# Attention loop of a hybrid diffusion step: row sums behind the first value visit, the inverse behind the fourth maximum, GpSimd's first addition behind two value products

## The chip, the cores and the metric

The kernel runs on one core of a Trainium2 chip. The metric is the device time of one execution, in microseconds (us). The median of three runs of the kernel before is 2347.97 us.

## The reference, cut to what matters

The reference is one layer of a hybrid backbone with three token mixers beside each other, followed by an output projection and a feed-forward part. The change touches only the attention mixer of the 1024 latent tokens. They are swept in 8 blocks of 128 queries; each block reads 1152 keys (1024 latent ones and 128 cached ones) with 8 query heads that share 2 key/value heads.

```python
def one(qblk):
    s = jnp.einsum('bqkgd,bskd->bkgqs', qblk, k).astype(jnp.float32) * scale
    p = jax.nn.softmax(s, axis=-1).astype(v.dtype)
    return jnp.einsum('bkgqs,bskd->bqkgd', p, v)
```

The softmax needs, for each query and head, a maximum over the keys, the exponentials, their sum (the row sum) and its inverse.

## The kernel before, in words

All work of the attention stage is in the function `attention` (L1876). Each engine has its own program, a list of instructions in a fixed order, and the engines meet only through semaphores. The order on each engine is written out by hand. The loop runs over tiles i = 0 to 7 (`LAST` is 7), one for each block of 128 queries. While tile i computes exponentials and products, TensorE already computes the scores that give the maxima of tile i + 1.

**TensorE** (`tile`, L2239). `head(h)` (`shift_scores`, three matmuls, L2165) fills PSUM banks 0 to 2 with the scores of head h of the next tile; it waits until the maximum of the head before has been taken. `steps` (`scores`, L2188 and L2189) makes the 18 transposed score blocks m = 0 to 17 of this tile, in three rotating banks, each freed by an exponential. `queries` and `shifts` (L2068 and L2073) turn the operands of a later tile through the one bank `PT`. `values(i, g)` (L2202) multiplies three blocks of exponentials with the values: this is one visit, there are three in a tile, and a visit has three products of two key/value heads each. `sums(i - 1)` (L2209) adds the exponentials of the previous tile over the keys, into the bank `PT`. `spread_sums(i - 1)` (L2235) spreads their inverse over the output rows. In the kernel before, `sums(i - 1)` stands between `head(2)` and `values(i, 0)`.

**VectorE** (`tile`, L2561). For each head it takes the maximum (L2531, reads PSUM). Between the maxima stand `next_split` (L2494 and L2495), which prepares the operands that `queries` turns; `norm_b` (L2489); `inverted` (L2537, the reciprocal of the row sums, reads the bank `PT`), in the kernel before after the third maximum (h = 2); `normed` (L2543) and `norm_a` (L2481, L2483, L2485) after the sixth; and in the last tile `ahead` (L2549, L2552), low parts of operands of the next stage.

**GpSimd** (`add_trio`, L2038). It adds the three blocks of exponentials a, b and c of a visit into c, so that TensorE has a third of the sums to make. The first addition (L2042) waits for the whole visit, the second (L2046) for the first, and in two visits of three also for a split of VectorE (`part`). Between the additions it runs `rope` (L2032 to L2035) and `inverse_norm` (L2023).

**ScalarE** (`tile`, L2388) takes the exponentials (L2379), copies turned operands out of `PT` (L2360, L2364), copies out the output (L2386), and in tiles 6 and 7 makes the high parts of operands of the next stage (`ahead`, L2409, L2412), after the exponentials 7, 13 and 17.

Who may write the bank `PT` is set by waits. The one that matters here is in `shifts`:

```python
if kv == 0 and i >= 2:
    pe.wait_ge(sem["rc"], i - 1)
```

Called as `shifts(i + 1, 0)` behind `head(4)`, it waits until `inverted(i - 1)` of this same tile has read the row sums.

Of the kernel before, what the change touches and what calls it, by code (L numbers as in the profile page):

```python
# [17 lines left out]
ALU = mybir.AluOpType  # L18
# [1857 lines left out]
def attention(nc, g):  # L1876
# [14 lines left out]
    TRIO, SLOTS = 3, 4  # L1891
    LASTG = (LAT // P) * NT // TRIO - 1
    LAST = LAT // P - 1
    fill = g.fill
    with Phase(nc, "att") as ph:
# [26 lines left out]
        ones, spread = ph.sb("ones", [P, 32]), ph.sb("spread", [P, G, HD])  # L1922
# [4 lines left out]
        with ExitStack() as later:  # L1927
            trio += [later.enter_context(nc.sbuf_tensor(f"att_trio{i}", [P, KV, G * P], F32)) for i in range(2, SLOTS)]
        b0st = [ph.sb(f"b0st{i}", [P, TH]) for i in range(STAGES)]
        names = ("load qload const knd kpow kout ktm kte qd qpow rope cpart qtm qte csmm cmx cex cptm cpte comm cdone "  # L1930
                 "part s1 mx ptm pte s2 ex pv paired sums rc spread norm evict yout0 yout1 kv dve mly mlw mlhi b0y1 b0y2 b0w b0yh b0wh b0yl b0wl b0mm b0ev b0out0 b0out1 b0out2 b0out3 b0out4 b0out5 b1lo")
        sem = {n: ph.sem(n) for n in names.split()}
        block = ph.block()
        PT, ST, OB = 3, 4, 7
# [1 line left out]
        def held(n):  # L1936

            b, r = divmod(n, TRIO)
            return trio[b % SLOTS] if r == TRIO - 1 else pt[b % 2 * 2 + r]
# [73 lines left out]
        @block.gpsimd  # L2013
        def _(gp):
            gp.memset(khalf[:], -0.5).then_inc(sem["const"], 1)
            gp.memset(va[:, :, :, HD:H1], 1.0).then_inc(sem["const"], 1)
            gp.memset(ones[:], 1.0).then_inc(sem["const"], 1)
            gp.wait_ge(sem["const"], 1)
            gp.wait_ge(sem["knd"], 3)
            gp.tensor_tensor(krs[:], kms[:], khalf[:], ALU.pow).then_inc(sem["kpow"], 1)  # L2020
            def inverse_norm(n):
                gp.wait_ge(sem["qd"], 4 * n + 3)
                gp.tensor_tensor(qrs[:], qms[:], khalf[:, 0:AH], ALU.pow).then_inc(sem["qpow"], 1)  # L2023

            def rope(n, e):

                gp.wait_ge(sem["qd"], 4 * n + 4 + 4)
                x = qn[:].rearrange("p h (d e) -> p h d e", e=2)
                o = qr[:].rearrange("p h (d e) -> p h d e", e=2)
                w = lambda c: qtab[:, n, c, :].unsqueeze(1).broadcast_to([P, AH, HD // 2])  # L2030
                a, b = (0, 1) if e == 0 else (2, 3)
                gp.tensor_tensor(u1[:], x[:, :, :, 0], w(a), ALU.mult).then_inc(sem["rope"], 1)  # L2032
                gp.tensor_tensor(u2[:], x[:, :, :, 1], w(b), ALU.mult).then_inc(sem["rope"], 1)
                gp.wait_ge(sem["rope"], 6 * n + 3 * e + 2)
                gp.tensor_tensor(o[:, :, :, e], u1[:], u2[:], ALU.subtract if e == 0 else ALU.add).then_inc(sem["rope"], 1)  # L2035
                gp.wait_ge(sem["rope"], 6 * n + 3 * e + 3)

            def add_trio(n, split=None):  # L2038

                a, b, c = (held(TRIO * n + x) for x in range(TRIO))  # L2040
                gp.wait_ge(sem["pv"], n + 1)
                gp.tensor_tensor(c[:], c[:], a[:], ALU.add).then_inc(sem["paired"], 1)  # L2042
                gp.wait_ge(sem["paired"], 2 * n + 1)
                if split is not None and split[0] <= LAST:
                    gp.wait_ge(sem["part"], 2 * split[0] + split[1] + 1)
                gp.tensor_tensor(c[:], c[:], b[:], ALU.add).then_inc(sem["paired"], 1)  # L2046

            inverse_norm(0)
            for n in range(2):
                inverse_norm(n + 1)  # L2050
                for e in range(2):
                    rope(n, e)
            inverse_norm(3)
            for i in range(LAST + 1):
                if i:
                    add_trio(3 * i - 1, (i + 1, 1))
                if i + 2 <= LAST:
                    rope(i + 2, 0)
                add_trio(3 * i)
                if i + 2 <= LAST:  # L2060
                    rope(i + 2, 1)
                add_trio(3 * i + 1, (i + 2, 0))
                if i + 3 <= LAST:
                    inverse_norm(i + 4)
# [12 lines left out]
        def _(pe):  # L2077
# [28 lines left out]
            n = 0  # L2106
            for part in range(2):
                rows = (P, H1)[part]
                for kv in range(KV):
                    for t0, nt in ((0, 4), (4, 4), (8, 2)):  # L2110
                        if n >= 6:
                            pe.wait_ge(sem["kte"], n - 5)
                        for t in range(nt):
                            mm = pe.transpose(ps[0:rows, n % 6, t * P:t * P + P],
                                              kpart[part][:, t0 + t, kv, :].bitcast(F32), g.ident[:])
# [75 lines left out]
            def values(i, g):  # L2191

                if g == 0:
                    if i:
                        pe.wait_ge(sem["evict"], i)
                    else:
                        pe.wait_ge(sem["b0ev"], 24)
                for j in range(TRIO * g, TRIO * g + TRIO):
                    n = NT * i + j
                    pe.wait_ge(sem["ex"], 2 * n + 2)  # L2200
                    for kv in range(KV):
                        mm = pe.matmul(ps[kv * HD:kv * HD + HD, OB, :], va[:, j, kv, 0:HD], held(n)[:, kv, :],  # L2202
                                       start=j == 0, stop=j == NT - 1)
                mm.then_inc(sem["pv"], 1)

            def add(x, first, last):
# [32 lines left out]
            def tile(i):  # L2239

                more = i < LAST

                def steps(first, last):
                    for m in range(first, last):
                        scores(i, m % KV, m // KV)

                def head(h):
                    if more:
                        shift_scores(i + 1, h)

                shifts(i, 1)
                head(0)
                steps(0, 4)
                head(1)
                if more:
                    queries(i + 1, 1)
                steps(4, 7)
                head(2)
                if i:
                    sums(i - 1)  # L2260
                values(i, 0)
                head(3)
                steps(7, 11)
                head(4)
                if more:
                    shifts(i + 1, 0)
                steps(11, 14)
                head(5)
                if i:
                    spread_sums(i - 1)  # L2270
                values(i, 1)
                head(6)
                steps(14, 18)
                head(7)
                if i + 2 <= LAST:
                    queries(i + 2, 0)
                values(i, 2)
# [29 lines left out]
        def _(act):  # L2307
# [80 lines left out]
            def tile(i):  # L2388
                more = i < LAST
                shifts(i, 1)  # L2390
                for m in range(2 * NT):
                    if more and m == 4:
                        queries(i + 1, 1)
                    if more and m == 11:
                        shifts(i + 1, 0)
                    exponentials(i, m // KV, m % KV)
                    if i >= LAST - 1 and m in (7, 13, 17):
                        ahead(3 * (i - LAST + 1) + (7, 13, 17).index(m))
                if i + 2 <= LAST:
                    queries(i + 2, 0)  # L2400
                output(i)

            def ahead(n):
                if n == 0:
                    act.wait_ge(sem["mly"], 64)
                if n == 4:
                    act.wait_ge(sem["mlw"], 32)
                if n < 4:
                    act.activation(g.ys0[:, n, :], g.ys0[:, 4 + n, :].bitcast(F32), ACT.Copy).then_inc(sem["mlhi"], 1)  # L2409
                else:  # L2410
                    b = n - 4
                    act.activation(g.wt[:, b, :], g.wraw[:, 2048 * b:2048 * b + 2048], ACT.Copy).then_inc(sem["mlhi"], 1)  # L2412
# [15 lines left out]
        def _(v):  # L2428
# [132 lines left out]
            def tile(i):  # L2561

                if i == -1:
                    norm_a(3)
                for h in range(AH):
                    if i < LAST:
                        shift(i + 1, h)
                    if 0 <= i < LAST and h == 0:
                        next_split(i + 1, 1)
                    if 0 <= i < NT - 3 and h == 1:  # L2570
                        norm_b(i + 3)
                    if i == LAST and h in (0, 1, 2):
                        ahead(h)
                    if i >= 1 and h == 2:
                        inverted(i - 1)
                    if i == LAST and h == 3:
                        ahead(3)
                    if i >= 1 and h == 5:
                        normed(i - 1)
                    if 0 <= i < NT - 4 and h == 5:  # L2580
                        norm_a(i + 4)
                    if i + 2 <= LAST and h == 6:
                        next_split(i + 2, 0)
# [1318 lines left out]
```

## Time and profile before

| | before |
|---|---|
| median of three runs | 2347.97 us (2347.4 to 2350.04) |
| the profiled execution, device time | 2346.06 us |
| its span in the trace | 2344.3 us |
| TensorE busy | 2264.6 us, 97% of the span |
| VectorE busy | 1401.5 us, 60% |
| ScalarE busy | 802.6 us, 34% |
| GpSimd busy | 337.0 us, 14% |
| attention tiles 0 to 7 | about 1157 to 1365 us of the span |

TensorE is the engine that is busy nearly all the time; the others work beside it. "PE" is TensorE's matmuls, "PEld" its weight loads, which run ahead of the matmuls and show well where TensorE stands in its program. "DVE" is VectorE, "ACT" ScalarE, "POOL" GpSimd. The time that an execution takes outside the span is 2346.06 - 2344.3 = 1.8 us.

### The profile page before, as it was taken

The page shows a single profiled execution, that of the slowest core. Times are in us where ns is not written, and L with a number is a line of the kernel's source. Part 1 is how long each engine was busy: PE and PEld are TensorE (multiplying, and loading weights), DVE is VectorE, ACT ScalarE, POOL GpSimd, SP SyncE. Part 2 cuts the span into 40 slices and gives each one's busy share as a digit, 9 for nine tenths or more (in the row PEclk, how much of TensorE's full clock was granted, in tenths as well). Part 3 has the DMA queues.
Part 4 walks back from the last instruction along what each step waited for, and adds up shares of the span by engine and source line. Part 5 has one row for each costly group of instructions (what it writes and reads, how often), then busy time and mean ns, then how long its engine had stood idle before and what let it go on. Part 6 is the DMA issues. An engine that isn't in the chain of part 4 may idle for free. (4 is left out here: it accounts for less than half of the span.)

```text
span 2344.3 us, 42939 instructions
## 1 busy us (share of the span) xinstructions
PE 2264.6 (97%) x17607; PEld 2025.9 (86%) x17607; DVE 1401.5 (60%) x2116; ACT 802.6 (34%) x1398; POOL 337.0 (14%) x291
## 2 busy tenths in 40 slices
PE   6999999999999999999999989998999999999997
PEld 5887779999999888999766679878999999998886
DVE  4341266543555466775576646668766766667877
ACT  5321123222333233323444544324332323234444
POOL 0000000001110011011377631000211211110001
PEclk9999999999999999999999999999999999999999
DMA  6325632327443523324201058321231232258534
GB/s 282 122 86 184 227 113 95 115 94 244 157 154 104 196 80 102 104 66 148 62 19 68 37 203 287 116 82 51 98 110 69 79 113 85 79 194 261 135 96 124
DMA packets 126874, 295.55 MB, mean 126 GB/s; under 512 B 19808, under 2 KB 63280, under 8 KB 117376
## 3 DMA queue, kind: packets, MB, share of 16 engines
q1 hardware_dynamic: 98112, 238.67, 30.5%
q10 hardware_dynamic: 24640, 39.46, 4.6%
q0 software_dynamic: 3968, 15.21, 1.7%
q8 instruction: 115, 1.88, 0.3%
q14 instruction: 39, 0.32, 0.0%
HBM read 207.83 MB, written 85.53 MB: 125 GB/s over the span
## 5 line engine op out<-in xcount | busy, mean ns | idle before, releaser
L62 PE MATMUL ps<-prj_w,h_hi 128*128 128x512 f32 (+1 forms) x864 | 255.3, 380 | 4.5 <-DVE h_lo L755 4.5
L62 PE MATMUL ps<-h_hi,fill_whi 128*128 128x384 f32 x672 | 235.4, 350 | 4.7 <-ACT fill_st L1119 2.4
L62 PE MATMUL ps<-wt 128*128 128x320 f32 (+2 forms) x1046 | 227.4, 327 | 2.5 <-DVE merged L3355 1.3
L62 PE MATMUL ps<-h_lo,fill_whi 128*128 128x384 f32 x672 | 226.0, 336 | 2.7 <-issue 2.7
L62 PE MATMUL ps<-h_hi,fill_wlo 128*128 128x384 f32 x672 | 226.2, 337 | 0.1
L62 PE MATMUL ps<-ys,mergedr 128*128 128x256 f32 (+1 forms) x1056 | 220.0, 297 | 0.4 <-issue 0.4
L62 PE MATMUL ps<-zb,mergedr 128*128 128x320 f32 (+2 forms) x764 | 199.7, 326 | 4.9 <-issue 2.7
L62 PE MATMUL ps<-zb,wt 128*128 128x384 f32 (+3 forms) x758 | 200.2, 325 | 0.0
L62 PEld LDWEIGHTS ps<-prj_w,h_hi 128*128 128x128 f32 x864 | 158.4, 191 | 42.9 <-issue 10.6
L62 PEld LDWEIGHTS ps<-wt 128*128 128x128 f32 x1046 | 179.5, 189 | 17.3 <-issue 2.6
L62 PEld LDWEIGHTS ps<-ys,mergedr 128*128 128x128 f32 x1056 | 174.7, 191 | 0.9 <-issue 0.9
L62 PE MATMUL ps<-prj_w,h_lo 128*128 128x512 f32 (+1 forms) x432 | 162.3, 376 | 0.0
L62 PE MATMUL ps<-xb,mergedr 128*128 128x320 f32 (+1 forms) x528 | 156.9, 297 | 0.0
L62 PE MATMUL ps<-ys,wt 128*128 128x384 f32 (+2 forms) x736 | 145.9, 320 | 6.2 <-DVE xf L3255 3.1
L62 PEld LDWEIGHTS ps<-zb,mergedr 128*128 128x128 f32 x764 | 136.5, 190 | 15.0 <-issue 4.6
L62 PEld LDWEIGHTS ps<-zb,wt 128*128 128x128 f32 x758 | 138.9, 189 | 4.5
L1119 ACT ACTIVATE fill_st<-ps 128x384 f32<-128x384 f32 x84 | 41.1, 490 | 278.7 <-PE ps L62 254.0
L62 PEld LDWEIGHTS ps<-h_hi,fill_whi 128*128 128x128 f32 x672 | 127.0, 189 | 7.6 <-ACT fill_st L1119 3.1
L62 PEld LDWEIGHTS ps<-ys,wt 128*128 128x128 f32 x736 | 125.6, 190 | 7.9 <-issue 3.9
L62 PEld LDWEIGHTS ps<-h_hi,fill_wlo 128*128 128x128 f32 x672 | 126.9, 189 | 2.8 <-issue 2.8
L62 PEld LDWEIGHTS ps<-h_lo,fill_whi 128*128 128x128 f32 x672 | 127.3, 189 | 0.0
L2531 DVE TENSOR_REDUCE att_qpart<-ps 128x1 fp32r<-128x1152 f32 x64 | 86.8, 1356 | 66.7 <-PE ps L2165 66.2
(513 smaller groups left out, 4701.9 us busy)
## 6 DMA issues: line engine op xcount, KB each, us to landing
wraw<-in_w_ffn_in SPq DMA_DIRECT2D x22, 1024.0 KB, 5.3
prj_raw<-in_w_ada SPq DMA_DIRECT2D x16, 1024.0 KB, 5.8
fill_raw<-in_w_fill SPq DMA_DIRECT2D x30, 512.0 KB, 4.5
wtf<-a_dram SPq DMA_DIRECT2D x55, 256.0 KB, 2.6
bg_dram<-fill_st ACTq DMA_DIRECT2D x72, 192.0 KB, 2.0
xf<-bg_dram POOLq DMA_DIRECT2D x24, 576.0 KB, 7.6
tok_dram<-prj_tst ACTq DMA_DIRECT2D x45, 256.0 KB, 2.1
prj_raw<-in_w_tok SPq DMA_DIRECT2D x10, 1024.0 KB, 7.3
```

Source lines behind the costliest of these rows:

```text
L62: mm = pe.matmul(out, lhs[a], rhs[b], start=first and n == 0, stop=last and n == 2, skip_group_check=onto)
L1119: act.activation(self.stage[t], self.g.ps[:, self.bank(u), 0:TH], ACT.Copy).then_inc(self.ev, 1)
L2531: v.tensor_reduce(qpart[kv][:, a, 0:1], ps[:, 0:3, 0:TH], AX.XY, ALU.max, negate=True).then_inc(sem["mx"], 1)
```

## The change: what it does

On TensorE `sums(i - 1)` moves from before to behind `values(i, 0)`. On VectorE `inverted(i - 1)` moves from behind the maximum h = 2 to behind h = 3. A new semaphore `duo` is raised by the second product of each visit. GpSimd's first addition now waits for `duo` in place of `pv`, and adds a into b; the second waits for `pv` and adds b into c. On ScalarE the first of the three `ahead` copies in tiles 6 and 7 moves from behind exponential 7 to behind exponential 6.

```diff
             def add_trio(n, split=None):
 
                 a, b, c = (held(TRIO * n + x) for x in range(TRIO))
+                gp.wait_ge(sem["duo"], n + 1)
+                gp.tensor_tensor(b[:], b[:], a[:], ALU.add).then_inc(sem["paired"], 1)
+                gp.wait_ge(sem["paired"], 2 * n + 1)
                 gp.wait_ge(sem["pv"], n + 1)
-                gp.tensor_tensor(c[:], c[:], a[:], ALU.add).then_inc(sem["paired"], 1)
-                gp.wait_ge(sem["paired"], 2 * n + 1)
                 if split is not None and split[0] <= LAST:
                     gp.wait_ge(sem["part"], 2 * split[0] + split[1] + 1)
                 gp.tensor_tensor(c[:], c[:], b[:], ALU.add).then_inc(sem["paired"], 1)
@@ 
                         mm = pe.matmul(ps[kv * HD:kv * HD + HD, OB, :], va[:, j, kv, 0:HD], held(n)[:, kv, :],
                                        start=j == 0, stop=j == NT - 1)
+                    if j % TRIO == 1:
+                        mm.then_inc(sem["duo"], 1)
                 mm.then_inc(sem["pv"], 1)
@@ 
                 head(2)
+                values(i, 0)
                 if i:
                     sums(i - 1)
-                values(i, 0)
                 head(3)
@@ 
-                    if i >= LAST - 1 and m in (7, 13, 17):
-                        ahead(3 * (i - LAST + 1) + (7, 13, 17).index(m))
+                    if i >= LAST - 1 and m in (6, 13, 17):
+                        ahead(3 * (i - LAST + 1) + (6, 13, 17).index(m))
@@ 
-                    if i >= 1 and h == 2:
+                    if i >= 1 and h == 3:
                         inverted(i - 1)
```

## Rows read from the trace of the kernel before

**Rows 1.** The page, busy time of TensorE: us, share of the span, instructions.
```profile
PE 2264.6 (97%) x17607; PEld 2025.9 (86%) x17607; DVE 1401.5 (60%) x2116; ACT 802.6 (34%) x1398; POOL 337.0 (14%) x291
```

**Rows 2.** Busy us (instructions) by stretch: PE, PEld, DVE, ACT, POOL; granted clock; DMA.
```profile
1240.00:1270.00 30.00, 29.78 (x237) 19.59 (x237) 22.05 (x22) 14.29 (x27) 23.30 (x16) 1.00 0.08 21
```

**Rows 3.** Timeline, tile 2, fourth head (last row: tile 3): start, duration, instruction, [idle before].
```profile
1215.82 1.25 PEld L2209 LDWEIGHTS ps<-att_trio,att_ones 128*32 128x32 f32 x48 [0.26 <-issue]
...
1217.27 0.20 PEld L2202 LDWEIGHTS ps<-att_pt,att_va 128*64 128x64 f32 x4 [0.20 <-issue]
...
1217.46 1.74 DVE L2537 RECIPROCAL att_rs<-ps 128x256 f32<-128x256 f32 x1
...
1220.00 0.47 PEld L2165 LDWEIGHTS ps<-att_kthi,att_qt 128*128 128x128 f32 x3 [0.81 <-issue]
...
1220.82 1.36 DVE L2531 TENSOR_REDUCE att_qpart<-ps 128x1 fp32r<-128x1152 f32 x1 [1.62 <-PE ps L2165]
...
1222.87 0.53 PEld L2073 LDWEIGHTS ps<-ident,att_qpart 128*65 128x65 f32 x4
1223.04 0.60 PE L2073 MATMUL ps<-ident,att_qpart 128*65 128x128 f32 x4
...
1224.66 0.61 PEld L2165 LDWEIGHTS ps<-att_kthi,att_qt 128*128 128x128 f32 x3
...
1243.71 1.74 DVE L2537 RECIPROCAL att_rs<-ps 128x256 f32<-128x256 f32 x1
```

**Rows 4.** Timeline, tile 2 from its second value visit to its last turn.
```profile
1226.34 0.25 PEld L2202 LDWEIGHTS ps<-att_pt,att_va 128*64 128x64 f32 x4
...
1228.94 0.17 DVE L2485 TENSOR_SCALAR att_qms<-att_qss 128x8 f32<-128x8 f32 x1
1229.12 0.47 PEld L2165 LDWEIGHTS ps<-att_kthi,att_qt 128*128 128x128 f32 x3 [0.81 <-issue]
...
1229.35 2.39 POOL L2042 TENSOR_TENSOR att_trio<-att_trio,att_pt 128x1024 f32<-128x1024 f32 x1 [2.03 <-PE ps L2202]
...
1229.95 1.36 DVE L2531 TENSOR_REDUCE att_qpart<-ps 128x1 fp32r<-128x1152 f32 x1 [0.84 <-PE ps L2165]
...
1231.22 0.68 DVE L2494 CAST att_qpart<-att_qr 128x256 fp32r<-128x256 f32 x1
...
1232.43 0.42 PEld L2068 LDWEIGHTS ps<-ident,att_qpart 128*128 128x128 f32 x4 [0.36 <-issue]
```

**Rows 5.** Timeline, the same place in tile 0.
```profile
1172.58 0.20 PEld L2202 LDWEIGHTS ps<-att_pt,att_va 128*64 128x64 f32 x4 [0.25 <-ACT att_pt L2379]
...
1175.53 2.40 POOL L2042 TENSOR_TENSOR att_trio<-att_trio,att_pt 128x1024 f32<-128x1024 f32 x1 [1.19 <-PE ps L2202]
1175.64 2.31 DVE L2485 TENSOR_SCALAR att_qms<-att_qss 128x8 f32<-128x8 f32 x1
...
1177.87 1.34 DVE L2531 TENSOR_REDUCE att_qpart<-ps 128x1 fp32r<-128x1152 f32 x1
...
1179.27 0.47 PEld L2165 LDWEIGHTS ps<-att_kthi,att_qt 128*128 128x128 f32 x3 [1.66 <-DVE att_qpart L2531]
...
1179.99 0.42 PEld L2068 LDWEIGHTS ps<-ident,att_qpart 128*128 128x128 f32 x4 [0.25 <-issue]
```

**Rows 6.** Timeline, tile 7.
```profile
1345.82 0.38 PEld L2209 LDWEIGHTS ps<-att_trio,att_ones 128*32 128x32 f32 x16 [0.74 <-POOL att_trio L2046]
...
1350.39 1.15 ACT L2409 ACTIVATE ys<-ys 128x1152 fp32r<-128x1152 f32 x1
...
1352.09 0.19 PEld L2188 LDWEIGHTS ps<-att_qt,att_kthi 128*128 128x128 f32 x1 [1.24 <-ACT att_pt L2379]
...
1356.31 2.29 DVE L2552 TENSOR_TENSOR wt<-wraw,wt 128x2048 fp32r<-128x2048 f32 x1 [0.77 <-ACT wt L2412]
...
1357.48 3.37 POOL L2042 TENSOR_TENSOR att_trio<-att_trio,att_pt 128x1024 f32<-128x1024 f32 x1 [2.30 <-PE ps L2202]
...
1363.35 0.38 PEld L2209 LDWEIGHTS ps<-att_trio,att_ones 128*32 128x32 f32 x16 [0.80 <-POOL att_trio L2046]
```

More of the change, by code:

```diff
@@ L1930, in attention @@
         names = ("load qload const knd kpow kout ktm kte qd qpow rope cpart qtm qte csmm cmx cex cptm cpte comm cdone "
-                 "part s1 mx ptm pte s2 ex pv paired sums rc spread norm evict yout0 yout1 kv dve mly mlw mlhi b0y1 b0y2 b0w b0yh b0wh b0yl b0wl b0mm b0ev b0out0 b0out1 b0out2 b0out3 b0out4 b0out5 b1lo")
+                 "part s1 mx ptm pte s2 ex duo pv paired sums rc spread norm evict yout0 yout1 kv dve mly mlw mlhi b0y1 b0y2 b0w b0yh b0wh b0yl b0wl b0mm b0ev b0out0 b0out1 b0out2 b0out3 b0out4 b0out5 b1lo")
         sem = {n: ph.sem(n) for n in names.split()}
```

## The prediction

> **What bounds the kernel now.** I read the page first: TensorE is busy for 97% of the span, every other engine for 60% or less [rows 1]. Then the busy time by stretch: in 30 us in the middle of the attention loop TensorE's matmuls leave 0.22 us free [rows 2]. So the loop runs at TensorE's own pace, and two things follow. There is next to nothing to gain in the middle of the loop, and there is no slack that could absorb a new stall of TensorE: whatever it has to wait is added to the time. Last the timeline of one ordinary tile, of tile 0 and of tile 7, for where TensorE does stand still and what comes 1 us later on each engine [rows 3 to 6]. In a timeline I read TensorE's place from its weight loads: the distance between two of them is what TensorE needs for the work between.
>
> **The change part by part.** I write H for the first load of `head(3)` in a tile, V for that of its second value visit; in tile 2 H is 1220.00 and V is 1226.34 [rows 3, 4].
>
> *Sums behind values.* The sums start at 1215.82, the visit at 1217.27, H is 1220.00: 1.45 and 2.73 us [rows 3]. The same work in the other order again ends at H, 4.18 us after the start. Nothing of it goes away. The three changes of tile shape (head, sums, values, head) are as many as before, of other pairs; I cost them at zero, with 0.3 us either way for a tile as the bound, about the 0.26 and 0.20 us of idle loads ahead of sums and values [rows 3]. The wait of the sums for GpSimd costs nothing in ordinary tiles (the idle before them is 0.26 us and names no other engine), so moving it away there gains nothing.
>
> *The inverse behind the fourth maximum.* The maximum of `head(3)` starts at 1220.82, H + 0.82, and takes 1.36 us [rows 3]; the instruction behind a maximum starts 0.09 us before the maximum's listed end (the CAST at 1231.22) [rows 4], so the reciprocal starts at H + 2.09. It takes 1.74 us [rows 3] and ends at H + 3.83. Before it ended at 1219.20, ahead of H. Who waits for it: `shifts(i + 1, 0)`, which may write `PT` only then. TensorE comes to it at 1222.87 with its first load and 1223.04 with its first matmul, H + 2.87 and H + 3.04 [rows 3]. Where TensorE waits for VectorE it starts shortly after VectorE ends (1179.27 after 1177.87 + 1.34 = 1179.21) [rows 5]; with 0.1 us for it that is H + 3.93 now, and the load that else runs ahead stands with its matmul. That is 1.06 us late by the load and 0.9 us by the matmul; matmuls are what fills TensorE's time, so I take 0.92 us. Behind it in TensorE's queue stands everything: scores 11 to 13, `head(5)`, `spread_sums`, the second visit. The wait is in tiles 1 to 6 (it needs i >= 1 and a next tile): 6 x 0.92 = **+5.5 us**. The maximum behind the reciprocal ends at about H + 3.8 + 1.4 = H + 5.2; `head(5)`, which needs it, would start at 1224.66, H + 4.66 [rows 3], and with the stall at H + 5.6. So this adds nothing more. The bounds are 0 (the wait is covered by something I do not see) and 6 x 1.06 = 6.4 us.
>
> *The first addition behind two products.* A visit lasts from V to `head(6)` at 1229.12, 2.78 us [rows 4]; a third of it is 0.93 us, and I take 0.9 us for how much earlier `duo` comes than `pv`. The first addition of the second visit starts at V + 3.0 now [rows 4], so at V + 2.1 after. Meanwhile VectorE runs `norm_a`, whose last and tiny instruction L2485 is at V + 2.6 [rows 4]. Tile 0 shows what happens when L2485 comes behind the start of an addition: started 0.11 us after it, it took 2.31 us in place of 0.17 us and ended with it, and the next maximum began only then [rows 5]. After the change this is so in each of tiles 1 to 4, which run `norm_a`: the addition runs from V + 2.1 to V + 4.5, the next maximum starts at V + 4.5 in place of 1229.95, V + 3.61 [rows 4]. From there to the load of the turn `queries` tile 0 has 1179.99 - 1177.87 = 2.12 us, maximum, CAST and subtraction behind each other [rows 5]. So the turn comes at V + 6.6, where it is at 1232.43, V + 6.09, now [rows 4]: 4 x 0.5 = **+2.0 us**. In tile 0 the addition that is in the way starts and ends 0.9 us earlier: **-0.9 us**. In tile 5, which has no `norm_a`, the CAST is held as in tile 2, where it ends at 1231.90, right behind the addition's 1231.74, and the turn behind it stands 0.36 us idle [rows 4]; there the earlier addition frees it: **-0.35 us**. In the third visit GpSimd comes to the addition from its own work in tiles 0 to 4, later than either semaphore, so nothing moves. If L2485 slipped in ahead of the addition, tiles 1 to 4 would gain those 0.36 us each instead, and tile 0, whose turn is at V + 7.4 [rows 5], would come to V + 5.7 like them, 1.7 us: 4 x 0.36 + 1.7 + 0.35 = 3.5. The bounds of this whole part are -3.5 us and, if tiles 0 and 5 gain nothing, +2.0 us.
>
> One page bears on this. The Trainium skill, "SBUF — State Buffer", section "Who interferes with whom", says that VectorE in a two-port mode (tensor_scalar and cast can be in one) and GpSimd lock each other out, and whoever issues first holds the ports for its whole instruction. Tile 0's 2.31 us agrees, and the rule speaks against the change in tiles 1 to 4 as above; if there were no lock, this part would gain.
>
> *Tile 7 and ScalarE's copy.* Here the sums do stand still for GpSimd, 0.74 us [rows 6]; behind the visit, 2.7 us later, they find it done: -0.7 us. The copy of `ahead` between exponentials 7 and 8 takes 1.15 us, and TensorE stands 1.24 us for an exponential behind it [rows 6]; I take 1.0 of them as the copy's. Behind exponential 6 it lies beside the visit and the sums, while ScalarE has nothing to do: -1.0 us. Together **-1.7 us**. In tile 6 the same copy costs next to nothing now, and the new wait for the reciprocal covers it. The stall of 0.80 us in the last sums stays: the addition there is held by L2552 of VectorE (it takes 3.37 us, from 1357.48, beside an instruction that runs from 1356.31 to 1358.60), and L2552 comes as much earlier as TensorE does [rows 6]. The reciprocal of tile 7 then ends at about 1350.3, and `spread_sums(6)`, which needs it, stands behind the score that is at 1352.09 now, 1350.4 after: no wait.
>
> **The sum.** +5.5 + 2.0 - 0.9 - 0.35 - 1.7 = +4.5 us. The profiled execution took 2346.06 us (span 2344.3, 1.8 us around it), 1.9 us under the median of the runs. It would become 2350.6 us; on the median, 2347.97 + 4.5 = **2352.5 us**. What this kernel's measurement can tell from no change is about 0.2%, 4.7 us: the forecast lies just within it.
>
> **Rivals.**
> - *Only the wait for the reciprocal is new.* L2485 gets in ahead of the addition, as it would if the second product's semaphore reached GpSimd 0.5 us later than I think (V + 2.6 decides). Then the second part is worth up to -3.5 in place of +0.75: 5.5 - 3.5 - 1.7 = +0.3, **2348.3 us**. Against it: the margin is 0.5 us of a time that follows TensorE's own pace. For it: only one row shows the collision.
> - *Only the lock is new.* The turn does not wait for the reciprocal: 4.5 - 5.5 = -1.0, **2347.0 us**. It would need VectorE to reach and finish the reciprocal 0.9 us earlier than the row of `head(3)`'s maximum allows.
> - *Neither is new*: 0.3 - 5.5 = -5.2, **2342.8 us**. This is the side on which the change is faster; it decides at the same two points.
> - *The reciprocal is locked out by GpSimd's additions (clearly slower).* The two additions of the first visit now run from about H - 1.4 to H + 3.5, over the reciprocal's place. If they held it as they hold L2485, it would end at H + 3.3 + 1.7 = H + 5.0, 1.2 us later, in 6 tiles: +7 more, **2359.7 us**. It decides on whether an instruction that reads PSUM can be held. Against it: the maxima, which read PSUM too, keep 1.36 us beside additions [rows 4]. The page named above says the same of instructions with at most one SBUF input outside the two-port modes.
> - *The new shape changes cost.* Values to sums and sums to head cost 0.3 us more than before in 7 tiles: +2.1, **2354.6 us**.
>
> **Chances.** The forecast 0.50; only the reciprocal 0.15; only the lock 0.10; neither 0.07; reciprocal locked 0.06; shape changes 0.12. The forecast lies so near the bound that I split it evenly, and of "neither" most is beyond the bound. Slower by over 0.2%: 0.25 + 0.06 + 0.12 = 0.43. Within 0.2%: 0.25 + 0.15 + 0.10 + 0.01 = 0.51. Faster: 0.06. The range takes in the forecast, both one-wait cases and the shape changes, and leaves out 0.13: 2346.5 to 2355.5 us. The likeliest case's own range is 2351 to 2354.
>
> **What the profile after would show.** Step 1: the load of L2073 behind `head(4)` in tiles 1 to 6 with about 1 us idle, released by the reciprocal, H + 3.9. Step 2: nine-tenths of a microsecond less wait of GpSimd's first addition for L2202; L2485 at over 2 us in tiles 0 to 4; a head (the eighth) that waits for a maximum in each of them, five such waits of 0.7 to 0.8 us where tile 0 alone had one, of 1.66 us [rows 5]. Step 3: no wait of the sums in tile 7 but for the last ones, and no 1.24 us wait for ScalarE. The tile period, 1243.71 - 1217.46 = 26.25 us now from one reciprocal to the next [rows 3], should be 27.7 us in tiles 2 to 4. The prediction is wrong if that period stays, or if it grows by more than 2 us.

## The result and the profile after

The changed kernel takes 2352.15 us (median of 22 runs, 2349.69 to 2355.99); the kernel before, on the same chips, 2347.27 us (22 runs). The ratio is 1.0023, with a 95% interval of 1.0017 to 1.0029: slower by 4.9 us, clear of noise. The forecast was +4.5 us and 2352.5 us. The profiled execution has a span of 2348.7 us, 4.4 us more than before.

In what follows lines of `kernel.py` are those of the changed kernel, up to three higher than before: L2166 is `head`, L2069 and L2074 the turns, L2189 the scores, L2203 the visits, L2212 the sums, L2042 and L2047 the additions, L2488 the tiny instruction of `norm_a`, L2540 the reciprocal. Beside [rows 1] the page now says, in the same columns:

```profile
PE 2265.2 (96%) x17607; PEld 2025.5 (86%) x17607; DVE 1405.4 (60%) x2116; ACT 802.2 (34%) x1398; POOL 337.2 (14%) x291
```

The work is the same (TensorE 0.6 us more busy); the time is waiting. The waits of the changed kernel from 1160 to 1375 us: who waited for whom, total us, times, longest us.

```profile
PE ps L2074 <- DVE att_rs L2540: 4.7, 6, 0.8
PEld ps L2166 <- DVE att_qpart L2534: 4.0, 5, 0.8
...
PEld ps L2212 <- POOL att_trio L2047: 0.8, 1, 0.8
```

Both new waits are here with the counts that the prediction gave: six turns wait for the reciprocal, five heads wait for a maximum. The sums wait for GpSimd once, where they did twice. The next fence is the timeline of tile 2 around its fourth head, the place of [rows 3].

```profile
1216.35 0.20 PEld L2203 LDWEIGHTS ps<-att_pt,att_va 128*64 128x64 f32 x4 [0.25 <-issue]
...
1219.07 1.25 PEld L2212 LDWEIGHTS ps<-att_trio,att_ones 128*32 128x32 f32 x48 [0.81 <-issue]
...
1220.52 0.48 PEld L2166 LDWEIGHTS ps<-att_kthi,att_qt 128*128 128x128 f32 x3 [0.20 <-issue]
...
1221.36 1.36 DVE L2534 TENSOR_REDUCE att_qpart<-ps 128x1 fp32r<-128x1152 f32 x1 [3.29 <-PE ps L2166]
...
1222.64 1.75 DVE L2540 RECIPROCAL att_rs<-ps 128x256 f32<-128x256 f32 x1
...
1224.50 0.41 PEld L2074 LDWEIGHTS ps<-ident,att_qpart 128*65 128x65 f32 x4 [1.08 <-issue]
1224.53 0.62 PE L2074 MATMUL ps<-ident,att_qpart 128*65 128x128 f32 x4 [0.79 <-DVE att_rs L2540]
...
1226.17 0.61 PEld L2166 LDWEIGHTS ps<-att_kthi,att_qt 128*128 128x128 f32 x3
```

H is 1220.52. Visit and sums together take 1220.52 - 1216.35 = 4.17 us, where the other order took 4.18 us [rows 3]: the new sequence costs nothing. The 0.81 us for which the load queue stands idle behind a visit is only in another place, ahead of the sums and no longer ahead of the head. The reciprocal ends at 1224.39, H + 3.87, and the turn's first load is at H + 3.98, where it was at H + 2.87. The idle of 1.08 us on the load queue carries the name "issue", but the matmul row beside it names the reciprocal. That matmul is at H + 4.01, where it was at H + 3.04 [rows 3]. From H to the load of `head(5)` it is now 5.65 us, 0.99 us more than in [rows 3].

Tile 2 from its second visit on, the place of [rows 4]:

```profile
1227.85 0.25 PEld L2203 LDWEIGHTS ps<-att_pt,att_va 128*64 128x64 f32 x4
...
1230.00 2.38 POOL L2042 TENSOR_TENSOR att_pt<-att_pt 128x1024 f32<-128x1024 f32 x1 [3.74 <-PE ps L2203]
1230.45 1.97 DVE L2488 TENSOR_SCALAR att_qms<-att_qss 128x8 f32<-128x8 f32 x1
...
1232.33 1.34 DVE L2534 TENSOR_REDUCE att_qpart<-ps 128x1 fp32r<-128x1152 f32 x1
...
1233.60 0.28 DVE L2497 CAST att_qpart<-att_qr 128x256 fp32r<-128x256 f32 x1
1233.73 0.47 PEld L2166 LDWEIGHTS ps<-att_kthi,att_qt 128*128 128x128 f32 x3 [0.79 <-DVE att_qpart L2534]
...
1234.40 0.42 PEld L2069 LDWEIGHTS ps<-ident,att_qpart 128*128 128x128 f32 x4 [0.20 <-issue]
```

V is 1227.85. The addition starts at V + 2.15, L2488 comes 0.45 us behind it, takes 1.97 us where it took 0.17, and ends with it. The maximum starts at V + 4.48, the turn at V + 6.55, where it was at V + 6.09. In tile 0, the place of [rows 5], the same wait ends 0.9 us earlier against the visit (V is 1172.47):

```profile
1175.29 1.69 DVE L2488 TENSOR_SCALAR att_qms<-att_qss 128x8 f32<-128x8 f32 x1
...
1176.90 1.34 DVE L2534 TENSOR_REDUCE att_qpart<-ps 128x1 fp32r<-128x1152 f32 x1
...
1179.02 0.42 PEld L2069 LDWEIGHTS ps<-ident,att_qpart 128*128 128x128 f32 x4 [0.26 <-issue]
```

And tile 7, the place of [rows 6]:

```profile
1351.08 0.20 PEld L2203 LDWEIGHTS ps<-att_pt,att_va 128*64 128x64 f32 x4 [0.36 <-issue]
...
1353.81 1.25 PEld L2212 LDWEIGHTS ps<-att_trio,att_ones 128*32 128x32 f32 x48 [0.81 <-issue]
1355.25 0.19 PEld L2189 LDWEIGHTS ps<-att_qt,att_kthi 128*128 128x128 f32 x1 [0.20 <-issue]
...
1361.76 4.20 POOL L2042 TENSOR_TENSOR att_pt<-att_pt 128x1024 f32<-128x1024 f32 x1 [3.57 <-PE ps L2203]
...
1368.45 0.38 PEld L2212 LDWEIGHTS ps<-att_trio,att_ones 128*32 128x32 f32 x16 [0.76 <-POOL att_trio L2047]
...
1369.68 0.46 PEld L2212 LDWEIGHTS ps<-att_trio,att_ones 128*32 128x32 f32 x16
```

The first sums run through without a wait for GpSimd, the 1.24 us for an exponential is gone, and the last sums still stand 0.76 us for GpSimd. Its addition came earlier (V + 2.09 where it was V + 2.95; V is 1359.67 here and was 1354.53), but it fell closer behind the start of a long subtraction of VectorE, and took 4.20 us in place of 3.37.

### The profile page after: what moved, and what is told of

Same layout as the page of the kernel before. It is cut to its first block and busy times, and to the rows that moved or that the text cites. A ratio compares the mean times of both kernels' runs of the same rounds, so it can differ in the third digit from the quotient of the medians.

```text
span 2348.7 us, 42950 instructions
## 1 busy us (share of the span) xinstructions
PE 2265.2 (96%) x17607; PEld 2025.5 (86%) x17607; DVE 1405.4 (60%) x2116; ACT 802.2 (34%) x1398; POOL 337.2 (14%) x291
```

## The experiments

My theory, A: the loss is two new waits of TensorE, for the reciprocal that now ends behind the turn (six tiles), and for a maximum behind the instruction that the earlier addition locks out (tiles 1 to 4); ScalarE's copy and the sums of tile 7 give 1.7 us back. The rivals: B, the earlier addition is the whole loss; C, the new sequence of tile shapes is. Rivals D, E and F are stated with the experiments that test them.

A run's device time moves by some 3 us to either side from one execution to the next, and much of that lies outside the loop: the first value visit starts anywhere from 1162.9 to 1166.4 us in the ten profiles, though nothing ahead of it differs in the programs. So beside the medians (22 runs of the changed kernel, 6 to 12 of each other) I give a length from each trace: from the first load of the first value visit to the last group of loads of the last sums. In the kernel before it is 1364.58 - 1164.32 = 200.26 us. There is one trace of each kernel, so how far this length can be trusted must be seen from like stretches: the kernel with ScalarE's copy alone has the program of before up to tile 6, and counted from the first visit each of its visits up to there starts within 0.05 us of where it did before.

| kernel | median, us | median of before in the same runs | difference | ratio, 95% interval | length of the loop, difference |
|---|---|---|---|---|---|
| changed | 2352.15 | 2347.27 | +4.9 | 1.0017 to 1.0029 | 205.45, +5.19 |
| sums and inverse alone | 2351.96 | 2347.14 | +4.8 | 1.0009 to 1.0027 | 205.36, +5.10 |
| addition alone | 2348.15 | 2347.14 | +1.0 | 0.9993 to 1.0010 | 201.14, +0.88 |
| ScalarE's copy alone | 2346.44 | 2347.14 | -0.7 | 0.9987 to 1.0004 | 199.11, -1.15 |
| copy for reciprocal | 2345.88 | 2347.14 | -1.3 | 0.9986 to 1.0003 | 199.62, -0.64 |
| inverse behind the third | 2352.62 | 2347.38 | +5.2 | 1.0012 to 1.0030 | 204.52, +4.26 |
| norm_a earlier | 2347.85 | 2347.38 | +0.5 | 0.9995 to 1.0012 | 201.26, +1.00 |
| mixed | 2341.58 | 2347.38 | -5.8 | 0.9967 to 0.9984 | 195.41, -4.85 |
| mixed, inverse_norm between | 2339.71 | 2347.38 | -7.7 | 0.9958 to 0.9981 | 193.87, -6.39 |

**Sums and inverse alone.** The kernel before with these two moves.

```diff
                 head(2)
+                values(i, 0)
                 if i:
                     sums(i - 1)
-                values(i, 0)
                 head(3)
...
-                    if i >= 1 and h == 2:
+                    if i >= 1 and h == 3:
                         inverted(i - 1)
```

> The kernel before with the sums behind the first visit and the inverse behind the fourth maximum, nothing else. Theory A (the turn in shifts waits for the later reciprocal, 0.92 us in each of tiles 1 to 6; the sums of tile 7 no longer stand 0.7 us for GpSimd): 5.5 - 0.7 = +4.8 us against the kernel before, with six waits of the turn for the reciprocal of about 0.8 us on the matmuls' side. Rival B (the earlier addition is what costs, through the ports it shares with VectorE): within 1 us of before. Rival C (the new sequence of tile shapes costs, not the reciprocal): about +5 too, but with the turn's wait absent and the distance from the head ahead of the sums to the head behind them longer than 5.04 us.

Measured +4.8 us, +5.10 in the loop. Its waits (lines as in the kernel before):

```profile
PE ps L2073 <- DVE att_rs L2537: 4.7, 6, 0.8
```

This is nearly all of the loss without any change on GpSimd, so B is out. From the head ahead of the visit to the head behind the sums tile 2 takes 5.03 us, where it took 5.04, and the turn does wait for the reciprocal: the sign that C needed is not there.

**Addition alone.** The kernel before with `duo`, a into b, b into c, as in the diff of the change.

```diff
+                gp.wait_ge(sem["duo"], n + 1)
+                gp.tensor_tensor(b[:], b[:], a[:], ALU.add).then_inc(sem["paired"], 1)
+                gp.wait_ge(sem["paired"], 2 * n + 1)
                 gp.wait_ge(sem["pv"], n + 1)
-                gp.tensor_tensor(c[:], c[:], a[:], ALU.add).then_inc(sem["paired"], 1)
-                gp.wait_ge(sem["paired"], 2 * n + 1)
```

> The kernel before with the first addition behind two value products, nothing else. Theory A: tiles 1 to 4 lose 0.5 us each because the tiny instruction of norm_a is caught behind the addition, tile 0 gains 0.9, tile 5 gains 0.35: +0.75 us, which a run can hardly tell from zero; in the trace the tiny instruction lasts about 2 us in tiles 0 to 4. Rival B (the addition is the whole loss): +4.9 us. Rival D (no lock, only gains): -3.5 us.

Measured +1.0 us with an interval that includes none; +0.88 in the loop. The time alone would prove little. The row of L2488 (line as in the changed kernel), its instructions over the whole kernel (durations ns, min/median/max), is what tells D from A:

```profile
L2488 DVE TENSOR_SCALAR att_qms<-att_qss x9: 170/1684/1966, 1111.3 to 1284.0; 128x8 f32<-128x8 f32 x9
```

Five of nine are held (the median itself is a held one); in the kernel before it was the one of tile 0.

**ScalarE's copy alone.**

```diff
-                    if i >= LAST - 1 and m in (7, 13, 17):
-                        ahead(3 * (i - LAST + 1) + (7, 13, 17).index(m))
+                    if i >= LAST - 1 and m in (6, 13, 17):
+                        ahead(3 * (i - LAST + 1) + (6, 13, 17).index(m))
```

> The kernel before with ScalarE's first copy of tiles 6 and 7 behind exponential 6 in place of 7, nothing else. Theory A: -1.0 us in tile 7 and -0.15 in tile 6, -1.15 us, and no 1.24 us wait of TensorE for an exponential in tile 7. If the copy is covered anyway: 0.

Measured -0.7 us, an interval that includes none, and -1.15 us in the loop, the two terms together. In tile 7 no score waits 1.24 us for an exponential now; the longest such wait of its loads is 0.24 us. The copy's place is what the 1.24 us hung on.

**A copy in place of the reciprocal.**

```diff
-                v.reciprocal(rs[:].rearrange("p k n -> p (k n)"), ps[:, PT, 0:KV * P]).then_inc(sem["rc"], 1)
+                v.tensor_copy(rs[:].rearrange("p k n -> p (k n)"), ps[:, PT, 0:KV * P]).then_inc(sem["rc"], 1)
```

> The changed kernel with a plain copy in place of the reciprocal, so the output is not divided by the row sums: the inverse is left out. A copy of 128x256 from PSUM should take about 0.4 us by the 0.68 us of normed for twice the size, so it ends at H + 2.5, ahead of the turn at H + 2.87. Theory A: the six waits go, 5.5 us under the changed kernel, that is -0.6 us against before. Rival C: no difference to the changed kernel, +4.9 us against before.

Measured -1.3 us against before, an interval that includes none, and 6 us under the changed kernel; -0.64 in the loop, 5.8 under the changed kernel. Tile 2:

```profile
1218.96 0.47 PEld L2166 LDWEIGHTS ps<-att_kthi,att_qt 128*128 128x128 f32 x3 [0.20 <-issue]
...
1221.07 0.41 DVE L2540 COPY att_rs<-ps 128x256 f32<-128x256 f32 x1
...
1221.85 0.53 PEld L2074 LDWEIGHTS ps<-ident,att_qpart 128*65 128x65 f32 x4
```

The same place on VectorE, the same order on TensorE, 0.41 us in place of 1.75, and the turn is back at H + 2.89. So the order of the sums costs nothing by itself, and C is out: what costs is the length of the instruction that stands between the fourth maximum and the turn.

**The inverse back behind the third maximum**, in the changed kernel.

```diff
-                    if i >= 1 and h == 3:
+                    if i >= 1 and h == 2:
                         inverted(i - 1)
```

> The changed kernel with the inverse back behind the third maximum; the sums stay behind the visit. The sums now end 0.2 us ahead of H, so the reciprocal runs from H to H + 1.7 and the fourth maximum starts behind it, at H + 1.65 in place of H + 0.82; head(4), which needs it, comes 0.75 us late, and the turn behind it no later than that. Theory A: 6 x 0.75 = 4.5 in place of 5.5: 1.0 us under the changed kernel, +3.9 us against before. Rival E (the place behind the fourth maximum is the mistake): all 5.5 us come back, -0.6 us against before.

The medians say +5.2 us, which is no less than the changed kernel's +4.9, but with intervals 4 and 3 us wide they can't tell 1 us; the loop says 0.93 us less than the changed kernel, near the 1.0 expected. Tile 2:

```profile
1219.64 0.47 PEld L2166 LDWEIGHTS ps<-att_kthi,att_qt 128*128 128x128 f32 x3 [0.20 <-issue]
...
1219.78 1.76 DVE L2540 RECIPROCAL att_rs<-ps 128x256 f32<-128x256 f32 x1 [2.58 <-PE ps L2212]
...
1221.45 1.29 DVE L2534 TENSOR_REDUCE att_qpart<-ps 128x1 fp32r<-128x1152 f32 x1
...
1222.86 0.47 PEld L2166 LDWEIGHTS ps<-att_kthi,att_qt 128*128 128x128 f32 x3 [0.98 <-issue]
1222.89 0.76 PE L2166 MATMUL ps<-att_kthi,att_qt 128*128 128x384 f32 x3 [0.57 <-DVE att_qpart L2534]
```

Here the reciprocal waits for the sums, holds the fourth maximum back, and `head(4)` comes at H + 3.22 in place of the H + 2.30 of the kernel before. Rival E is out: once the sums are behind the visit, either place stalls TensorE, and the one behind the fourth maximum does so by about 0.15 us a tile more. The choice that matters is the order on TensorE. Ahead of the visit, the sums give VectorE 2.7 us of visit under which to hide the reciprocal.

**norm_a earlier**, in the changed kernel.

```diff
+                    if 0 <= i < NT - 4 and h == 4:
+                        norm_a(i + 4)
                     if i >= 1 and h == 5:
                         normed(i - 1)
-                    if 0 <= i < NT - 4 and h == 5:
-                        norm_a(i + 4)
```

> The changed kernel with norm_a moved up from behind the sixth to behind the fifth maximum, so that its tiny instruction lies ahead of GpSimd's addition. Theory A: the lock goes in tiles 0 to 4 and the CAST is freed too: 4 x (0.5 + 0.36) + 0.8 = 4.2 us under the changed kernel, +0.7 us against before; the tiny instruction lasts 0.17 us, or under 1 us where a rope step of GpSimd is in the way. Rival F (the head's wait for the seventh maximum has another cause): no difference to the changed kernel, +4.9 us.

Measured +0.5 us against before, an interval that includes none, and 4.3 us under the changed kernel; +1.00 in the loop, 4.2 under the changed kernel, as expected. Tile 2:

```profile
1225.11 0.68 DVE L2484 TENSOR_TENSOR att_q<-att_q 128x512 f32<-128x512 f32 x1
1225.16 1.23 POOL L2035 TENSOR_TENSOR att_qr<-att_u 128x256 f32<-128x256 f32 x1
...
1226.54 0.17 DVE L2488 TENSOR_SCALAR att_qms<-att_qss 128x8 f32<-128x8 f32 x1
...
1229.58 2.38 POOL L2042 TENSOR_TENSOR att_pt<-att_pt 128x1024 f32<-128x1024 f32 x1 [3.20 <-PE ps L2203]
...
1233.14 0.53 PEld L2069 LDWEIGHTS ps<-ident,att_qpart 128*128 128x128 f32 x4
```

The tiny instruction is 3 us ahead of the addition and takes 0.17 us. The visit of this tile starts at 1227.43, so the turn is at V + 5.71, with no idle before it: 0.38 us earlier than in the kernel before, 0.84 earlier than in the changed one. F is out. The wait was the lock.

**Mixed.** If A is right, the parts can be had separately: sums ahead of the visit and inverse behind the third maximum as before, except in tile 7; the addition behind two products; `norm_a` behind the fifth maximum; ScalarE's copy behind exponential 6.

```diff
                 head(2)
-                if i:
+                if i and more:
                     sums(i - 1)
                 values(i, 0)
+                if i and not more:
+                    sums(i - 1)
                 head(3)
```

Here `more` is true in all tiles but the last. The other moves are those shown above: `duo`, `norm_a` and ScalarE's copy.

> What theory A says is good in the change, without what it says is bad: the sums ahead of the visit and the inverse behind the third maximum as before, but in tile 7 the sums behind the visit; the addition behind two products; norm_a behind the fifth maximum; ScalarE's copy behind exponential 6. Theory A: tiles 1 to 4 gain 0.36 each, tile 0 1.7, tile 5 0.35, tiles 6 and 7 1.85: -5.3 us against before. If norm_a collides with the second addition in its new place and delays the sixth maximum, or if the gains are given back elsewhere: between -1.9 and 0 us.

Measured -5.8 us, 2341.58 us, ratio 0.9976 (0.9967 to 0.9984); -4.85 us in the loop. It beats both kernels. In the loop it is 0.45 us short of the forecast, and most of that lies at one place: the turn of tiles 1 to 4 was to bring 0.36 us each, the idle time of its loads [rows 4], and from the second visit to the third these tiles gained 0.25 to 0.27 us.

**Mixed, with inverse_norm between the additions.** 

```diff
                 gp.tensor_tensor(b[:], b[:], a[:], ALU.add).then_inc(sem["paired"], 1)
+                if between is not None:
+                    inverse_norm(between)
...
-                    add_trio(3 * i - 1, (i + 1, 1))
+                    add_trio(3 * i - 1, (i + 1, 1), i + 3 if i + 2 <= LAST else None)
...
-                if i + 3 <= LAST:
-                    inverse_norm(i + 4)
```

> As the kernel with the mixed parts, and GpSimd's inverse_norm moved from ahead of the third visit's first addition to behind it, so that this addition starts with its semaphore and is over before the CAST of the next tile's first split. Theory A: the turn of queries(i + 1, 1), which stands 0.46 us for that split, comes 0.4 us earlier in tiles 1 to 5: 2.0 us under the mixed kernel, -7.3 us against before. If the split is not what the turn waits for: same as the mixed kernel.

Measured -7.7 us, 2339.71 us, ratio 0.9969 (0.9958 to 0.9981); -6.39 us in the loop, 1.5 us under the mixed kernel where 2.0 was expected. The split and the turn of tile 2, first in the mixed kernel:

```profile
1208.60 0.62 DVE L2499 CAST att_qpart<-att_qr 128x256 fp32r<-128x256 f32 x1
...
1209.79 0.42 PEld L2069 LDWEIGHTS ps<-ident,att_qpart 128*128 128x128 f32 x4 [0.35 <-issue]
1209.82 0.63 PE L2069 MATMUL ps<-ident,att_qpart 128*128 128x128 f32 x4
```

And with `inverse_norm` between the additions:

```profile
1208.40 0.28 DVE L2499 CAST att_qpart<-att_qr 128x256 fp32r<-128x256 f32 x1
...
1209.26 0.52 PEld L2069 LDWEIGHTS ps<-ident,att_qpart 128*128 128x128 f32 x4
...
1209.42 0.60 PE L2069 MATMUL ps<-ident,att_qpart 128*128 128x128 f32 x4
```

The CAST is not held and the turn has no idle before it. The third visit starts at 1203.38 in the one and at 1203.18 in the other; counted from it, the load is 0.33 us earlier, but the first matmul only 0.20. From one reciprocal to the next tiles 2 to 5 now take 25.63 or 25.64 us, where the mixed kernel took 25.88, 26.17, 25.92 and 25.87. So tiles 2, 4 and 5 gain about 0.25 us each and not 0.4, and tile 3 gains 0.3 more (the last section shows where that stood). The idle time of the loads was too high a price for this wait; the shift of the first matmul is nearer.

## Why the prediction was right, point by point

*Sums behind values at zero*: right, 4.17 for 4.18 us, and the copy in place of the reciprocal confirms it from the other side.

*The wait for the reciprocal, +5.5 us*: right in mechanism and place, with H + 3.98 for the forecast H + 3.93. From H to `head(5)` tile 2 loses 0.99 us where 0.92 was taken. In tile 6 the distance grows from 1329.39 - 1324.58 = 4.81 to 1336.19 - 1330.56 = 5.63 us, by 0.82, since the copy's small cost went under it as expected (with the sums and the inverse alone, where the copy is in its old place, it is 5.63 too). So the term is 5.8, 0.3 more. The price is the delay of the matmul, as the prediction chose: the turn's first matmul comes 4.01 - 3.04 = 0.97 us later, its load 1.11. The forecast of 0.9 was too small because the reciprocal ended 0.04 us later than reckoned and the matmul started 0.14 us behind it, where 0.1 was taken for the load.

*The first addition, +2.0, -0.9 and -0.35 us*: `duo` came at V + 2.15, V + 2.1 was forecast; the turn at V + 6.55, V + 6.6 was forecast: 4 x 0.46 = +1.8. Tile 0 gained 7.41 - 6.55 = 0.86. In tile 5 the load of the turn moved from V + 6.08 to V + 5.71, 0.37 us, but the third visit moved by 0.26 only. L2488 lasts 1.69 us in tile 0 and 1.97 in tiles 1 to 4, not the "over 2 us" that was to be seen: it starts 0.44 us or more behind the addition, not 0.11, and still ends with it. The single row of tile 0 was enough to see the collision in four others.

*Tile 7, -1.7 us*: from the start of the part that is reordered to the last sums it was 1364.58 - 1344.28 = 20.30 us and is 1369.68 - 1351.08 = 18.60. Right, and right too that the last wait of the sums stays, though the addition's stay on GpSimd grew by the whole head start.

*What the sum missed*: the loop grew by 5.19 us, not 4.5. The starts of the visits in the two traces say in which part:

| part | forecast, us | measured, us |
|---|---|---|
| wait for the reciprocal, tiles 1 to 6 (third visit before it to second visit) | +5.5 | +6.13, of it 0.3 in tile 3 |
| first addition, tiles 1 to 4 (second visit to third) | +2.0 | +1.89 |
| tile 0 up to its third visit | -0.9 | -0.88 |
| tile 5 (second visit to third) | -0.35 | -0.26 |
| tile 7 up to the last sums | -1.7 | -1.69 |

The parts add up to the 5.19 us. The mechanism was right in each; the term that was mis-sized is the first, by 0.3 us for the delay of the matmul and by 0.3 more in tile 3 alone, where a late second addition of GpSimd delays a turn (last section). The span grew by 4.4 only, as the part behind the loop was 0.7 us shorter in this execution (979.0 for 979.7), which has nothing to do with the change. That the forecast of 2352.5 us lies 0.35 us from the measured median is in part luck: it stands on the median of three runs, 2347.97 us, and the 22 runs of the kernel before gave 2347.27, which makes up for a change of +4.9 us where +4.5 was forecast.

*The rivals*: neither wait was covered; the reciprocal was not locked out by the additions over which it now lies (1.75 us for 1.74), which was the rival that would have cost 7 us more; the shapes cost nothing. *The chances*: I split the forecast evenly about the bound of 0.2%, and the measured 0.23% lies just beyond it; on which side it came to lie is luck. The bound was also wider than what the measurement can tell: with 22 runs of each kernel the interval is 0.06% to either side. By tile period, 27.7 us was forecast for tiles 2 to 4; from reciprocal to reciprocal it is 27.73, 28.00, 27.72 and 27.72.

## What to carry to other kernels

Here moving a step behind another on the engine that is never idle cost that engine nothing (4.17 us for 4.18), and what counted was what the step released: the sums had handed VectorE a 1.7 us instruction with 2.7 us of products over it, and afterwards it had none. Work out for each moved producer how long its consumer is and which instruction of the busy engine comes after it. And before starting an engine's work earlier, look at what short instruction of an engine that the trace has shown to be held by it comes behind the new start: here a 0.17 us instruction of VectorE lasted 1.97 us behind the addition and cost TensorE 0.46 us a tile, and moving `norm_a` out of the way brought 4.2 us. When you price such a wait, take the delay of the first matmul behind it and not the idle time of the loads, which said 1.08 us where 0.97 was lost and 0.36 where 0.25 was won.

## What the runs showed of the hardware that I had not expected

The lock, by which one of the two engines holds up an instruction of the other, works both ways. A VectorE multiplication with two operands in SBUF (L2484, 0.68 us) that starts first lengthens a rope step of GpSimd from 0.73 to 1.23 us; in tile 7 an addition of 2.4 us grows to 4.20 us beside a subtraction of 2.29 that started 0.33 us ahead of it (to 3.37 us in the kernel before, where the subtraction had started 1.17 us ahead). The Trainium skill, "SBUF — State Buffer", section "Who interferes with whom", says that VectorE with two SBUF inputs contends with a GpSimd instruction that reads SBUF; both rows agree.

At the end of tile 2, in the changed kernel, GpSimd takes up the second addition 0.30 us later than in tiles 1, 3 and 4. The row in question, and its neighbour in tile 3:

```profile
1234.81 2.35 POOL L2047 TENSOR_TENSOR att_trio<-att_trio,att_pt 128x1024 f32<-128x1024 f32 x1 [2.42 <-DVE att_qpart L2498]
...
1262.49 2.35 POOL L2047 TENSOR_TENSOR att_trio<-att_trio,att_pt 128x1024 f32<-128x1024 f32 x1 [2.12 <-DVE att_qpart L2498]
```

The same 0.3 us stands at the same place in all seven kernels with the new first addition and in none of the three with the old one, so it belongs to the program and not to the execution. It costs TensorE 0.3 us in the turn of tile 3, but not in the last kernel, where the third visit's first addition starts with its semaphore. What it is stays open.
